# Reading the chunk state with one 128-column product per group and head pair

## The reference, cut to what matters

```
def wkv7_scan(r, w, k, v, a, b):
    # S_t = S_{t-1} diag(w_t) + (S_{t-1} a_t) b_t^T + v_t k_t^T ;  y_t = S_t r_t
    def step(state, inp):
        r_t, w_t, k_t, v_t, a_t, b_t = inp
        sa = einsum('bhvk,bhk->bhv', state, a_t)
        state = state*w_t[:, :, None, :] + sa[..., None]*b_t[:, :, None, :] + v_t[..., None]*k_t[:, :, None, :]
        y_t = einsum('bhvk,bhk->bhv', state, r_t)
        return state, y_t
    ...
y = wkv7_scan(r_h, w_h, k_h, v_h, -kk, kk * a_h)
```

## Time and profile before

| | |
|---|---|
| median of the runs | 1937.01 us |
| profiled execution, its own time | 1941.11 us |
| its span | 1938.6 us |
| TensorE busy | 1911.1 us (99% of the span) |
| DVE busy | 952.4 us |
| ACT busy | 780.2 us |
| mean granted TensorE clock | 0.999 |

### The profile page before, as it was taken

How to read it: one execution, slowest core, us unless ns; L and a number is a source line. 1 busy time by engine, 2 the same in 40 slices (tenths; PEclk the granted TensorE clock), 3 DMA queues, 4 the chain that set the end, 5 groups by cost and what they waited for, 6 DMA issues and landing times.

```text
span 1938.6 us, 29303 instructions
## 1 busy us (share of the span) xinstructions
PE 1911.1 (99%) x12106; PEld 1588.1 (82%) x12106; DVE 952.4 (49%) x1497; ACT 780.2 (40%) x1210; POOL 61.2 (3%) x119
## 2 busy tenths in 40 slices
PE   7999999999999999999999999999999999999998
PEld 5887778778788888888899978888888888888887
DVE  6548645375443344438733146544344544344446
ACT  6364545453432133245632252333422542133244
POOL 0000000000320000000001100000000000000000
PEclk9999999999999999999999999999999999999999
DMA  4322110024432333222322222222233322222222
GB/s 171 98 76 80 64 44 4 14 98 123 138 107 98 98 98 98 96 78 99 130 88 88 86 84 92 77 83 76 92 111 118 109 98 98 98 98 96 94 94 87
DMA packets 52648, 178.25 MB, mean 92 GB/s; under 512 B 7919, under 2 KB 8511, under 8 KB 52528
## 3 DMA queue, kind: packets, MB, share of 16 engines
q1 hardware_dynamic: 45328, 162.03, 25.1%
q0 software_dynamic: 6512, 13.34, 2.3%
q10 hardware_dynamic: 688, 1.11, 0.2%
HBM read 170.13 MB, written 5.47 MB: 91 GB/s over the span
## 4 chain that ended last, share of the span: by engine, by line
PE 94%; DVE 2%; ACT 2%; DMA 1%; issue 1%; ACTq 0%; SPq 0%
PE bank L696 92%; DMA ring<-in_stream 1%; DVE ring_lo L2046 1%; ACT work L1478 1%; PE bank L935 0%; PE bank L1036 0%; ACT ring_hi L1478 0%; DMA x<-in_xT 0%; PE bank L883 0%; DVE work L2502 0%; ACT L1478 0%; DVE x L2504 0%; PE bank L1408 0%; DVE work L2509 0%; PE bank L1411 0%
## 5 line engine op out<-in xcount | busy, mean ns | idle before, releaser
L696 PE MATMUL bank<-work_r,ring_hi 128*128 128x512 f32 x2608 | 815.8, 392 | 13.1 <-DVE ring_lo L2046 13.1
L2046 DVE TENSOR_TENSOR ring_lo<-ring,ring_hi 128x1024 fp32r<-128x1024 f32 x303 | 369.2, 1224 | 616.0 <-ACT ring_hi L1478 615.4
L696 PEld LDWEIGHTS bank<-work_r,ring_hi 128*128 128x128 f32 x2608 | 491.2, 188 | 116.9 <-DVE ring_lo L2046 13.8
L1478 ACT ACTIVATE ring_hi<-ring 128x1024 fp32r<-128x1024 f32 x303 | 319.1, 1056 | 527.0 <-DMA ring<-in_stream 524.8
L696 PE MATMUL bank<-work_r,ring_lo 128*128 128x512 f32 x1304 | 510.2, 391 | 0.0
L696 PE MATMUL bank<-h_hi,ring_hi 128*128 128x512 f32 (+1 forms) x872 | 341.7, 392 | 2.1 <-DVE ring_lo L2046 2.1
L696 PE MATMUL bank<-h_hi,ring_lo 128*128 128x512 f32 (+1 forms) x872 | 338.0, 388 | 0.0
L696 PEld LDWEIGHTS bank<-work_r,ring_lo 128*128 128x128 f32 x1304 | 246.4, 189 | 51.7 <-issue 1.0
L696 PE MATMUL bank<-h_lo,ring_hi 128*128 128x512 f32 (+1 forms) x872 | 215.9, 388 | 0.0
L696 PEld LDWEIGHTS bank<-h_hi,ring_hi 128*128 128x128 f32 x872 | 163.7, 188 | 42.1 <-issue 8.9
L696 PEld LDWEIGHTS bank<-h_hi,ring_lo 128*128 128x128 f32 x872 | 163.8, 188 | 34.0 <-issue 1.2
(11 more groups left out here) (245 smaller groups left out, 1509.1 us busy)
## 6 DMA issues: line engine op xcount, KB each, us to landing
ring<-in_stream SPq DMA_DIRECT2D x303, 512.0 KB, 3.3
x<-in_xT POOLq DMA_DIRECT2D x8, 256.0 KB, 3.0
spill<-x POOLq DMA_DIRECT2D x1, 2048.0 KB, 9.2
work<-x POOLq DMA_DIRECT2D x32, 64.0 KB, 2.2
x<-spill POOLq DMA_DIRECT2D x8, 256.0 KB, 2.9
rows<-work SPq DMA_DIRECT2D x8, 256.0 KB, 2.9
x<-in_xT ACTq DMA_DIRECT2D x2, 512.0 KB, 8.5
x<-in_xT SPq DMA_DIRECT2D x2, 512.0 KB, 7.1
```

The costliest lines, as they stand in the source:

```text
L696: ins = pe.matmul(out, lhsT, rhs, start=start, stop=stop, skip_group_check=True)
L1478: return nc.scalar.activation(out, in_, func, **kw)
L2046: v.tensor_tensor(ring_lo[:, n % RING, :, :], ring[:, n % RING, :, :], ring_hi[:, n % RING, :, :], ALU.subtract).then_inc(sem("split_lo"), 1)
```

## The change

`readers` and `local_outputs` become one job "ry" per chunk. For every m and g one product takes all 128 columns of `WG[g]` (64 left rows, 128 left columns), so that the reader comes out on 64 partitions and the first part of the local output on the other 64. A second product, of 64 by 64, adds the values' part to the latter 64 partitions. So that both groups g can be added and copied on the partitions where they belong, the two halves of `WG[1]` change places, and with them the operands of `solved`: the token-major tile of one operand moves to `x[:, 7, :]`, and the masked values of g = 1 take the tile 35. `W_AT` and `V_AT` say which half is which.

DVE adds the reader in two instructions of 64 partitions x 256 per chunk (four per tile), ACT copies the local output in two instructions of 64 x 256 per chunk. Both read one bank, and ACT waits for DVE's two additions (semaphore "reads") before it copies and frees the bank. TensorE's order: ry of chunk 0 where rr was; ry of chunk 1 where st and yl of chunk 0 were; st where yl of chunk 1 was. There are two jobs fewer per tile.

```diff
-            def readers(t):
-                for g in range(2):
-                    pe.wait_ge(*is_drained("LQ", t, g))
-                    pe.wait_ge(*is_drained("MQ", t, g))
-                jobs = both("rr", t)
-                outs = [take(*job) for job in jobs]
-                side_by_side(jobs, [(c, outs[c][rows(g), m * CH:(m + 1) * CH], WG[g][rows(c), m, 0:HN],
-                                     QB[t % 2][rows(c), g, m, :], True, True) for m in range(4) for c, g in CORNERS])
-
-            def local_outputs(t, c):
-                out = take("yl", t, c)
+            def readers(t, c):
+                if c == 0:
+                    for g in range(2):
+                        pe.wait_ge(*is_drained("LQ", t, g))
+                        pe.wait_ge(*is_drained("MQ", t, g))
+                out = parts(take("ry", t, c)[:, :])
                 steps = []
                 for m in range(4):
-                    steps += [(out[rows(g), m * CH:(m + 1) * CH], WG[g][rows(c), m, HN:P],
-                               QB[t % 2][rows(c), g, m, :], True, False) for g in range(2)]
-                    steps += [(out[rows(g), m * CH:(m + 1) * CH], head(tok(3, t), m, g)[rows(c), :],
-                               QK[t % 2][rows(c), g, m, :], False, True) for g in range(2)]
-                single(("yl", t, c), steps)
+                    for g in range(2):
+                        steps += [(out[:, g, m, :], WG[g][rows(c), m, :], QB[t % 2][rows(c), g, m, :], True, False),
+                                  (out[rows(1 - g), g, m, :], head(tok(3, t), m, g)[rows(c), :],
+                                   QK[t % 2][rows(c), g, m, :], False, True)]
+                single(("ry", t, c), steps)
...
-                    steps += [(out[rows(g), m, 0:HN], WG[g][rows(c), m, 0:HN], head(tok(1, t), m, g)[rows(c), :],
+                    steps += [(out[rows(g), m, 0:HN], WG[g][rows(c), m, W_AT[g]:W_AT[g] + HN], head(tok(1, t), m, g)[rows(c), :],
...
                 if t:
-                    if s:
-                        next_state(2 * s)
-                    local_outputs(s, 0)
+                    readers(s, 1)
...
                 wider(t, 3)
                 if t:
-                    local_outputs(s, 1)
+                    if s:
+                        next_state(2 * s)
                     turn_tile(2, t)
...
-                copy_half(grp(W(YL))[:, :, CH * c:CH * (c + 1)], "yl", t, c)
+                split_hi(blocks_to("ry", t, c))
+                act.wait_ge(*computed("ry", t, c))
+                act.wait_ge(sem("reads"), 4 * t + 2 * c + 2)
+                out = parts(bank(("ry", t, c))[:, :])
+                for g in range(2):
+                    here, there = slice(64 * g, 64 * g + 64), slice(64 - 64 * g, 128 - 64 * g)
+                    ins = f(grp(W(YL))[here, :, CH * c:CH * (c + 1)], out[there, g, :, :], ACT.Copy)
+                    ins.then_inc(*((act_step, tick()) if g == 0 else (bank_drained[nth("ry", t, c)], 1)))
...
+            def readers(t, c):
+                ch = 2 * t + c
+                split_lo(blocks_to("ry", t, c))
+                dve.wait_ge(*computed("ry", t, c))
+                out = parts(bank(("ry", t, c))[:, :])
+                for g in range(2):
+                    r = work[64 * g:64 * g + 64, R0:R0 + 4, ch * CH:(ch + 1) * CH]
+                    v.tensor_tensor(r, out[64 * g:64 * g + 64, g, :, :], r, ALU.add).then_inc(sem("reads"), 1)
```

More of the change, by code:

```diff
@@ L178, in chunk_jobs @@
     t = TT - 1
-    j += [SLICED] + both("w", t) + [MIDGATE] + both("gh", t) + both("rr", t) + both("yl", t)
+    j += [SLICED] + both("w", t) + [MIDGATE] + both("gh", t) + both("ry", t)
     return j + [("st", 2 * t)] + [("lg", m) for m in range(RT)] + [("yf", t)]
@@ L188, in beside @@
         return {1: [("tr", 1, 0), ("tr", 2, 0)], 2: [("tr", 3, 2), ("tr", 3, 3)], 3: [], 4: []}[n]
-    return {1: [("gh", s, 0)], 2: both("rr", s) + [("tr", 1, t)], 3: [("yl", s, 1), ("tr", 2, t)],
+    return {1: [("gh", s, 0)], 2: [("ry", s, 0), ("tr", 1, t)], 3: ([("st", 2 * s)] if s else []) + [("tr", 2, t)],
             4: both("mv", t) + [("tr", 0, t)]}[n]
@@ L200, in behind @@
         return both("mv", 0) + [("tr", 3, 1)] if n == 1 else []
-    return {1: [("gh", s, 1)], 2: ([("st", 2 * s)] if s else []) + [("yl", s, 0)], 4: [("yf", s), ("st", 2 * s + 1)]}[n]
+    return {1: [("gh", s, 1)], 2: [("ry", s, 1)], 4: [("yf", s), ("st", 2 * s + 1)]}[n]
 def late_gates():
@@ L466, in tok @@
         def tok(q, t):
-            return W({0: 36, 1: 38, 2: 35, 3: 39 + t}[q])
+            return x[:, 7, :] if q == 2 else W({0: 36, 1: 38, 3: 39 + t}[q])
         homes = [R0, R0 + 1, R0 + 2, R0 + 3, K0, K0 + 1, K0 + 2, K0 + 3, V0, V0 + 1, V0 + 2, V0 + 3, WDAD, GD]
@@ L489, in two_blocks @@
         TTP = [by_pair(bias[:, 3, :]), by_pair(W(11))]
-        MB, MVB = parts(nr[:, 0, :]), by_pair(W(37))
+        MB, MVB = parts(nr[:, 0, :]), [by_pair(W(37))[:, 0, :, :], by_pair(W(35))[:, 1, :, :]]
+        W_AT, V_AT = (0, HN), (HN, 0)
         QB, QK = [parts(W(45)), parts(W(43))], [parts(W(46)), parts(nr[:, 1, :])]
@@ L1057, in solved @@
                         steps += [(g, outs[g][rows(c), m, :], turned[rows(c), g, m, :],
-                                   work[rows(c), 36:38, n[g]], True, True) for c, g in phase]
+                                   work[rows(c), 36 - g:38 - g, n[g]], True, True) for c, g in phase]
                 side_by_side(jobs, steps)
@@ L1069, in chunk_updates @@
                 for m in range(4):
-                    steps += [(out[rows(g), m, 0:HN], WG[g][rows(c), m, 0:HN], head(tok(1, t), m, g)[rows(c), :],
+                    steps += [(out[rows(g), m, 0:HN], WG[g][rows(c), m, W_AT[g]:W_AT[g] + HN], head(tok(1, t), m, g)[rows(c), :],
                                True, True) for g in range(2)]
-                    steps += [(out[rows(g), m, HN:P], head(tok(1, t), m, g)[rows(c), :], WG[g][rows(c), m, HN:P],
+                    steps += [(out[rows(g), m, HN:P], head(tok(1, t), m, g)[rows(c), :], WG[g][rows(c), m, V_AT[g]:V_AT[g] + HN],
                                True, False) for g in range(2)]
@@ L1107, in from_states @@
                 for c in range(2):
-                    pe.wait_ge(*is_drained("rr", t, c))
+                    pe.wait_ge(sem("reads"), 4 * t + 2 * c + 2)
                     pe.wait_ge(*is_drained("gh", t, c))
@@ L1146, in _ @@
                 if t:
-                    readers(s)
+                    readers(s, 0)
                     turn_tile(1, t)
@@ L1192, in _ @@
             gate_third(MIDGATE, 1)
-            readers(TT - 1)
-            local_outputs(TT - 1, 0)
-            local_outputs(TT - 1, 1)
+            readers(TT - 1, 0)
+            readers(TT - 1, 1)
             gate_third(MIDGATE, 2)
@@ L1663, in copy_values @@
                 for g in range(2):
-                    copy_half(MVB[:, g, :, :], "mv", t, g)
+                    copy_half(MVB[g], "mv", t, g)
             def copy_solved(t):
@@ L2339, in outputs @@
                 for c in range(2):
-                    split_lo(blocks_to("yl", t, c))
-                    dve.wait_ge(*is_drained("yl", t, c))
+                    split_lo(blocks_to("ry", t, c))
+                    dve.wait_ge(*is_drained("ry", t, c))
                 split_lo(blocks_to("yf", t))
@@ L2365, in _ @@
                     chunk_updates(s, 1)
-                    readers(s)
+                    readers(s, 0)
                 off_diagonal(t, 3)
+                if t:
+                    readers(s, 1)
                 if s > 0:
```

## The result

The changed kernel takes 1990.99 us (median of 4 runs, 1990.6 to 1992.24), against 1937.13 us: the ratio is 1.0275, 95% interval 1.0263 to 1.0288, or +53.9 us. I had forecast +30 us and a range that ended at 1974. The direction is right, the size is not.

A forecast was written before the change was run, and what follows sets the result against it. TensorE was taken to bound the kernel, busy 99% of the span. +40.6 (new pairs) - 10.0 (old products) + 0.4 (entry) + 0.3 (uncovered wait) - 0.8 (issue waits) gave about +30 on 1937.0: 1967 us, range 1945 to 1974.

The forecast's parts named there:

- the array emptying between A and B: In ry, per (m, g), A (128 left columns) and B (64 by 64) drain between them: 0.635 us per pair, +40.6 us.
- the 10.0 us that go: The old rr and two yl jobs, 48 products per tile, removed from TensorE in four tiles: 10.0 us.
- rival 1: In ry, no emptying between A and B, the weight load binds: 5.4 us per tile, +11, 1948 us; chance 0.20.
- rival 4: The clock falls: at half clock a tile's two jobs take up to 10 us more, 40 us more, 2007 us; chance 0.04.
- The issue waits: TensorE's unexplained waits in dense streams of short records, 1.6 us; a slower stream may save half, -0.8 us.
- T of level 3: In the ladders yl no longer follows it; some 0.3 us shows once, 3 us in all if another 1 us were uncovered.
- DVE's four instructions: DVE's readers and ACT's copies go from 2 to 4, 0.35 to 0.4 us each: 0.7 us more per tile, hidden.
- Rivals 1, 2 and 3: The second: in ry no load binds, each record streams in 58 ns; 3.7 us per tile, +5, 1942 us; chance 0.05.
- rival 5: In ry, each change of shape costs a full 0.375 us visit for B too: +38, 1975 us; within the forecast's 0.63.
- rival 3: In ry the number of records counts, A and B overlapping: under 0.16 us per pair, -3.9, 1933 us; chance 0.08.

The follow-up runs named there:

- Experiment 1: The changed kernel with each 128-column product split into two of 64 left columns, so no shape changes inside a ry job: 1938.58 us, ratio 1.0005.
- experiment 2: The changed kernel with each job's products grouped by shape, all 64*128 first, then all 64*64; the values' product mostly replaces instead of adding: 1949.07 us, ratio 1.0059.
- Experiment 3: The changed kernel with m = 1 and 3 split into products of 64 left columns, halving the changes of shape: 1963.49 us, ratio 1.0132.
- experiment 8: The kernel of experiment 7, but ACT copies the first local output before the turned tile: 1982.72 us, ratio 1.0241.
- experiments 7: The changed kernel with eight unneeded 64*64 products in four corners added behind each of a job's first seven pairs: 1994.08 us, ratio 1.0287.
- Experiment 4: The changed kernel with both chunks in one job, 64*128 products alternating row halves, then 64*64 round four corners; values' product mostly replaces: 1946.89 us, ratio 1.0047.
- (9): The changed kernel with products of 64 left columns only, each job using one column half and then the other: 1948.0 us, ratio 1.0053.
- 6: The changed kernel grouped by shape, 64*64 products first and 64*128 added on top; only each half's first 64*64 product clears: 1952.54 us, one run.

## Why the prediction was wrong

**The mechanism was right, and measured.** I forecast the array emptying between A and B, 0.375 + 0.26 = 0.635 us per pair (the terms given for B add up to 0.27, not 0.26); it is 0.62. 64 pairs make 39.4 us where I had 40.6, for the 10.0 us that go. Experiment 1 shows that nothing else of the change costs, experiment 2 that without the alternation the same products cost +11. That this is also the figure of rival 1 is chance: the jobs of experiment 2 take 8 x 2.51 = 20.1 us, +10, and the rest goes with its lower clock in the last tile. "TensorEngine Tiling (Array Packing)" of the Trainium skill, Key Properties, which the forecast weighed, is borne out for the pair 64x128 and 64x64, that no row had shown.

**The step that failed is the clock.** The sum was made at full clock, and the fall stood beside it as rival 4, with a chance of 0.04 and a price of 40 us, as if it were a case apart. In the runs it comes with the forecast's own mechanism: experiment 1, without the alternation, has a clock of 1.00 throughout. From the three long stretches after, the time at half clock is 2 x (0.17 x 40 + 0.21 x 46 + 0.26 x 54) = 61 us. Of the time spent there, 1 - 0.615/1.015 = 39% would not be needed at full clock, if the other steps lose in the same proportion: 24 us. With the +29.4 that makes 53.6 us; measured are 53.9. The starts in the trace bear it out: the eight ry jobs take 6.15, 5.6, 5.3, 7.9, 5.6 and 7.9 us and 13.6 for the last two, 52 us in all, 12.6 more than the 39.4 at full clock; the other 12 us lie in ladder steps and the gate part behind the last tile. Experiment 3 repeats it at half the dose: 0.11 x 145 x 2 = 32 us at half clock, 12.6 us by the same share, and 32 pairs (8 x 3.2 - 10.0 = 15.6): 28 us, measured 25.7. The shares are estimates; that the clock takes part is shown by the rows and by the spread of experiment 8's runs, and the second and third tile of experiments 7 and 8 show that added work can hold it up.

**Why I gave it 4 in 100.** I argued from the page of before, where the clock was full, though its shortest pattern of this kind is one visit of four transposes between dense jobs. A full clock in dense work says nothing about work that I had myself computed to stream for a third of its time. And I read the price as two doubled jobs (10 us per tile): in the pair only 0.62 becomes 1.02, not 1.24, but the ladder steps behind the job pay as well, as the four transposes show.

**The other steps.** The issue waits fell from 1.6 to 0.3 us; I had taken off half, for a slower stream. That reason doesn't hold: in experiment 1, whose stream is dense, they are 0.4 us. T of level 3 is not uncovered by more than before: DVE and ACT as releasers stay at 2.4 us, under the 3.2 of before. DVE's four instructions take 422 ns each and ACT's 379, the price of a 128-partition one, and are hidden. Rivals 1, 2 and 3 are out by the 0.62 us per pair, and rival 5 by the 0.26 us of B. Experiment 4 reaches the 0.16 us per pair at which rival 3 begins, but only by sending the products to both row halves.

**What stays open.** What the clock follows is narrowed, not settled: one corner streaming without pause keeps it (9), pairs with an emptying before each don't (3), pairs with dense work between them do in the second and third tile, but not in all of the first tile and not at the end (7, 8). An idle stretch stands shortly before the first fall in experiments 4 and 7, and none in the changed kernel and in 8. The 3 us between experiments 2 and 6 rest on one run. The medians of experiments 7 and 8 lie 11.4 us apart (on two chips; 9.6 us when each is taken against the kernel before beside it), and what of it is the clock and what the removed wait was not told apart.

## What to carry to other kernels

Count small products by how many parts of the array run beside one another, not by their number: a tile's 32 products, each job in one row half and in two shapes, took 9.9 us at full clock (16 pairs of 0.62), where 48 of one shape took 2.55 us. Don't alternate left operands of different shape in one stream. Grouping them took the loss from 54 to 11 us (in a kernel whose values' product doesn't add; 14 us in one run of the one where it does), and splitting the wider one took it away. And when a change makes the array wait between short products, price the clock as part of it: the busy column stayed at 5.00 of 5.00 us here, and only the granted clock told.

## What the runs showed of the hardware

- A change between 64*128 and 64*64 left operands costs what an emptied array costs, in both directions: 0.36 and 0.26 us for two records each, against 0.22 and 0.12 by pace.
- Loads of 128 columns into the two row halves overlap: 64 records (32 of them with 128 left columns) in 2.56 us, against 2 x 2.51 with each chunk alone.
- In a run of such pairs (0.62 us each, against 0.34 by pace) the granted clock fell to 0.50 with TensorE shown as busy all the time; at half clock a pair takes 1.015 us, 1.65 times as long and not twice. The four transposes take 1.04 instead of 0.58 us.
- "PSUM — Partial Sum Buffer" of the Trainium skill, The four PSUM rules, says that the first product of a group clears the written marks of a whole zero region (the bank, on the partitions that the product writes), not only of the columns that it writes, and that a product that doesn't clear replaces where the mark is clear and adds where it is set. By it the values' products of experiments 2 and 4 replace, because another 64*128 product has cleared behind theirs, and the 64*128 products of experiment 6, where only the first 64*64 product of each half clears, add. No trace here shows the marks.
